# Depthwise convolution and silu moved into the input projection, and eight value-page buffers for four, in a hybrid decoder step

## The chip, the cores and the metric

The kernel runs on one core of a Trainium2 chip. The metric is the device time of one execution in microseconds, lower is better. Work is written for five engines by hand: TensorE (PE), VectorE (DVE), ScalarE (ACT), GpSimd (POOL) and SyncE (SP). Each has its own queue of instructions in program order; semaphores are the only order between queues.

## The reference

One layer of a hybrid decoder for 512 prompt tokens and 8 sample sequences of 8 tokens (576 columns, T), all in float32. The parts that the change touches:

```python
u = x @ w_in      # -> q | k | v | forget logits | z | xBC | dt | gate_att | gate_ssm
# depthwise causal convolution over 4 taps, 4096 channels; buf: the last 3 columns before
xp = concat([buf, xbc]); y = b
for j in range(4): y = y + w[j] * xp[:, j:j + l]
xbc, new_buf = silu(y), xp[:, l:]
xs, bm, cm = split(xbc)                 # 2048 | 8 groups x 128 | 8 groups x 128
y, h_new = ssd(xs, dt, a, bm, cm, h0)   # Mamba-2 state space part
m = grouped_rms_norm((y + d_skip * xs) * silu(z)) * norm_w
# sample attention reads 16 pages of 128 keys and values per sequence from a paged cache
```

Then both branches are merged through gates and an output projection, with layer norms, and PEER retrieves 128 experts per token. All states, keys, values and `new_buf` are outputs.

## The kernel before

Tensors are kept transposed: 128 channels on the partitions, 576 tokens along a row. `build` (L2397) runs four stages one after another, each in a block of its own: `project_and_prompt` (L95), `mamba_and_samples` (L653), `front` (L1356) and `peer`.

**Projection.** `u` is made in 97 tiles of 128 channels. A tile's weights (1 MB) are loaded by SP into a ring of four, ScalarE rounds them (L345), DVE takes the remainder (L470), TensorE makes 96 matmuls of 288 columns (L246), and ScalarE and DVE evict one half each (L357, L476) into a ring of four `out` buffers, which GpSimd stores to `uT` in DRAM (L620). The first 17 tiles (misc, q, k) are written out; the other 80 run in 4 rounds of 20 slots, body(r, t). In four slots of five a step of prompt attention lies between the products: scores (L277), mask and maximum on DVE (L542 to L546), exponential on ScalarE (L402), division on DVE (L554), transposes and values (L285, L295). On DVE a slot is: maximum, weight remainder, division, eviction. On ScalarE: exponential, rounding of the next weights, copy of transposes, head loads, eviction. The convolution isn't done here.

**Fused stage.** Eight groups g of the Mamba part (chunks c of 128 tokens) are interleaved by hand with the attention of sample sequence g. Per group SP loads four raw tiles (two of x, one of B, one of C, `load_raw` L791), the running sums, z and the old state, double-buffered by g % 2. DVE makes the edges of the sample sequences (`conv_edges` L909) and convolves the four tiles of group g + 1 one at a time at fixed places inside group g (`conv` L922): tile 2 ahead of `after_matrix(g, 2)`, tile 3 after `after_matrix(g, 4)`, tile 0 between the sample states 1 and 2, tile 1 ahead of `mean_square(g)`. ScalarE's `conv` (L1146) does silu of these tiles in that order, then silu of z, and only then the scaling of the attention output (L1189), for which TensorE's `turn_out` (L1322) waits. TensorE's order within a group is: scores of 16 key pages (L1281) among the chunks' products (L1222 to L1234), transposes (L1291), values 0 to 3 (L1306), chunk 4, values 4 to 7, sample states 0 and 1 (L1246), values 8 to 11, sample states 2 and 3, values 12 to 15, the square sums (L1255), `turn_out`, and the first scores of the next group (L1264).

GpSimd gathers pages of 512 KB by indirect DMA: six buffers for keys (RK), four for values (RV). Its order is

```python
for c in range(RK, PAGES): page_k(b, c)
for c in range(8): page_v(b, c)
if more:
    for c in range(RK): page_k(b + 1, c)
for c in range(8, PAGES): page_v(b, c)
```

and a gather waits until its buffer's last page is used (`k_used`, `v_used`).

## Time and profile before

| | us |
|---|---|
| median of 3 runs | 5410.88 (5408.63 to 5411.28) |
| the profiled execution | 5412.87 |
| its span, first to last instruction | 5411.1 |
| projection, from the first product to the last head's output | 13.4 to 1484.6 |
| fused stage | 1498 to 2192 |
| merge stage | 2192 to 2968 |
| PEER | 2968 to 5411 |

| engine | busy us | share of the span |
|---|---|---|
| TensorE | 4053.6 | 75% |
| VectorE | 3325.7 | 61% |
| ScalarE | 849.1 | 16% |
| GpSimd | 1463.3 | 27% |

The page cuts the span into 40 slices of 135 us. Each digit is a busy share in tenths; PEclk is the granted TensorE clock in tenths.

```profile
PE   9999999999957777899999999999999900000000
DVE  2322222222257766433452897878879789999998
PEclk9999999999967777899999999999999955555555
DMA  4332323232177876534564999999999999999998
```

The projection fills the first eleven slices, with TensorE full; the fused stage is slices 11 to 16, where no engine is full.

### The profile page before, as it was taken

What the parts mean: (1) busy time and instruction counts of PE and PEld (TensorE: products, weight loads), DVE (VectorE), ACT (ScalarE), POOL (GpSimd) and SP (SyncE); (2) the same over time, 40 slices, a digit from 0 to 9 for tenths busy, and PEclk for the clock granted to TensorE, in tenths of its full rate; (3) what the DMA queues carried; (4) which work ended last, traced back from release to release, by engine and by line L of the source; (5) the groups of instructions that cost most, each with busy time, mean ns of one, the idle gap of its engine ahead of it and who ended that gap; (6) DMA issues with size and microseconds to landing.
All of it is one profiled execution on the core that took longest, in us unless ns stands there. A gap on an engine that the chain in (4) does not pass through costs nothing. (4 is left out here: it accounts for less than half of the span.)

```text
span 5411.1 us, 60657 instructions
## 1 busy us (share of the span) xinstructions
PE 4053.6 (75%) x24165; PEld 3236.8 (60%) x24165; DVE 3325.7 (61%) x4454; ACT 849.1 (16%) x1210; POOL 1463.3 (27%) x1609
## 2 busy tenths in 40 slices
PE   9999999999957777899999999999999900000000
PEld 7999999999935545798798555555555500000000
DVE  2322222222257766433452897878879789999998
ACT  2212221212112222322352000000000000000000
POOL 0000000000043333000010122222222367777774
PEclk9999999999967777899999999999999955555555
DMA  4332323232177876534564999999999999999998
GB/s 156 117 126 100 106 100 105 100 106 100 57 254 271 289 278 241 196 110 169 173 211 161 355 419 419 398 418 421 421 420 419 421 379 410 410 410 409 410 410 331
DMA packets 336652, 1462.02 MB, mean 270 GB/s; under 512 B 84452, under 2 KB 113028, under 8 KB 196600
## 3 DMA queue, kind: packets, MB, share of 16 engines
q0 software_dynamic: 174304, 995.20, 46.1%
q1 hardware_dynamic: 131304, 430.86, 22.0%
q10 hardware_dynamic: 30768, 32.11, 1.8%
q8 instruction: 194, 3.18, 0.2%
q14 instruction: 82, 0.67, 0.0%
HBM read 1362.71 MB, written 94.75 MB: 269 GB/s over the span
## 5 line engine op out<-in xcount | busy, mean ns | idle before, releaser
L2231 DVE SCALAR_TENSOR_TENSOR i_acc<-i_row,i_cf,i_acc 128x2048 f32<-128x2048 f32 x571 | 1344.8, 2355 | 156.1 <-DMA i_row<-in_expert_v,i_ei 119.3
L2038 PE MATMUL i_p_h<-i_xT,i_ut 128*128 128x384 f32 x4096 | 1322.4, 486 | 0.0
L2038 PEld LDWEIGHTS i_p_h<-i_xT,i_ut 128*128 128x128 f32 x4096 | 779.1, 190 | 540.9 <-issue 0.6
L2347 POOL DMA_INDIRECT i_row<-in_expert_v,i_ei x576 | 544.9, 946 | 633.7 <-DVE i_acc L2231 512.2
L246 PE MATMUL a_acc<-a_xh,a_wh 128*128 128x288 f32 x3104 | 672.2, 298 | 18.1 <-DVE a_xl L466 13.4
L246 PE MATMUL a_acc<-a_xh,a_wl 128*128 128x288 f32 x3104 | 665.2, 296 | 0.0
L246 PE MATMUL a_acc<-a_xl,a_wh 128*128 128x288 f32 x3104 | 664.8, 296 | 0.0
L246 PEld LDWEIGHTS a_acc<-a_xh,a_wh 128*128 128x128 f32 x3104 | 499.2, 189 | 29.6 <-issue 26.0
L2222 DVE CUSTOM_DVE_ANT_0 i_row<-i_row,i_acc 128x2048 f32<-128x2048 f32 x192 | 433.5, 2286 | 125.1 <-DMA i_row<-in_expert_u,i_ei 123.3
L246 PEld LDWEIGHTS a_acc<-a_xl,a_wh 128*128 128x128 f32 x3104 | 500.4, 189 | 0.0
L246 PEld LDWEIGHTS a_acc<-a_xh,a_wl 128*128 128x128 f32 x3104 | 500.3, 189 | 0.0
L476 DVE COPY a_out<-a_acc 128x288 f32<-128x288 f32 x97 | 44.4, 457 | 732.8 <-PE a_acc L246 732.8
L470 DVE TENSOR_TENSOR a_wl<-a_w,a_wh 128x2048 fp32r<-128x2048 f32 x105 | 240.7, 2292 | 300.4 <-ACT a_wh L345 183.5
L2352 POOL DMA_INDIRECT i_hs<-tmp_Ha,i_hx x384 | 369.2, 961 | 117.5 <-issue 117.5
L1704 DVE TENSOR_TENSOR f_wl<-f_w,f_wh 128x1024 fp32r<-128x1024 f32 x176 | 207.7, 1221 | 221.2 <-ACT f_wh L1592 219.6
L2347 POOL DMA_INDIRECT i_row<-in_expert_u,i_ei x192 | 182.3, 949 | 560.4 <-DVE i_hs L2222 454.8
L620 POOL DMA_DIRECT2D tmp_uT<-a_out x80 | 43.7, 546 | 1040.4 <-DVE a_out L476 1026.0
L2070 ACT COPY i_ho<-i_p_h 128x384 f32<-128x384 f32 x128 | 61.2, 478 | 1248.8 <-PE i_p_h L2038 1248.8
L1592 ACT CAST f_wh<-f_w 128x1024 fp32r<-128x1024 f32 x176 | 176.1, 1049 | 379.6 <-PE f_acc L1516 210.6
L875 POOL DMA_INDIRECT e_kr<-in_cache_k,e_ik x128 | 128.1, 1001 | 201.7 <-PE e_ps L1281 173.7
L882 POOL DMA_INDIRECT e_vr<-in_cache_v,e_ik x128 | 121.2, 947 | 198.2 <-PE e_ps L1306 174.1
L357 ACT COPY a_out<-a_acc 128x288 f32<-128x288 f32 x80 | 31.9, 398 | 820.6 <-PE a_acc L246 820.6
(310 smaller groups left out, 5450.9 us busy)
## 6 DMA issues: line engine op xcount, KB each, us to landing
i_ut<-in_u_tiles SPq DMA_DIRECT2D x128, 1024.0 KB, 9.7
a_w<-in_w_in SPq DMA_DIRECT2D x97, 1024.0 KB, 4.8
f_w<-in_w_out SPq DMA_DIRECT2D x32, 1024.0 KB, 5.1
f_w<-in_w_query SPq DMA_DIRECT2D x32, 1024.0 KB, 5.2
tmp_uT<-a_out POOLq DMA_DIRECT2D x97, 288.0 KB, 2.4
tmp_Ha<-i_ho ACTq DMA_DIRECT2D x128, 192.0 KB, 9.2
f_w<-in_w_bs SPq DMA_DIRECT2D x16, 1024.0 KB, 4.9
c_csb<-tmp_cs SPq DMA_DIRECT2D x32, 288.0 KB, 5.8
```

The costliest lines, as they stand in the source:

```text
L246: last = nc.tensor.matmul(acc[:, 2 * slot + h, 0:HALF], weights[:, wslot, k * P:(k + 1) * P], x[:, k, h * HALF:(h + 1) * HALF], start=(k = ...
L470: v.tensor_tensor(wl[:, it % 2, :], w[:, it % RING, :], wh[:, it % 2, :], ALU.subtract).then_inc(w_split, 1)
L875: pool.indirect_dma_start(kr[:, n % RK, :], None, io["cache_k"], bass.IndirectOffsetOnAxis(ik[:, n:n + 1], axis=0)).then_inc(k_in[n % RK], 16)
L882: pool.indirect_dma_start(vr[:, n % RV, :], None, io["cache_v"], bass.IndirectOffsetOnAxis(ik[:, n:n + 1], axis=0)).then_inc(v_in[n % RV], 16)
L1592: nc.scalar.copy(wh[:, i % 2, h * W // 2:(h + 1) * W // 2], w[:, i % RW, h * W // 2:(h + 1) * W // 2]).then_inc(wh_out, 1)
L1704: last = v.tensor_tensor(wl[:, i % RW, part], w[:, i % RW, part], wh[:, i % 2, part], ALU.subtract)
L2038: last = nc.tensor.matmul(p_h[:, e % 2, 0:ND], ut[:, e % RU, k * P:(k + 1) * P], xT[:, k, :], start=(k == 0), stop=(k == KT - 1))
L2070: nc.scalar.copy(ho[:, m, :], p_h[:, e % 2, 0:ND]).then_inc(h_out, 1)
L2222: v.tensor_tensor_reduce(row[:, m % R, :], row[:, m % R, :], acc, 1.0, 0.0, ALU.mult, ALU.add, hs[:, j, k:k + 1]).then_inc(row_used, 1)
L2231: v.scalar_tensor_tensor(acc, row[:, m % R, :], cf[:, j, k:k + 1], acc, ALU.mult, ALU.add).then_inc(row_used, 1)
L2347: pool.indirect_dma_start(row[:, m % R, :], None, table, bass.IndirectOffsetOnAxis(index, axis=0)).then_inc(row_in[m % R], 16)
L2352: pool.indirect_dma_start(hs[:, j, k:k + 1], None, h_flat, bass.IndirectOffsetOnAxis(hx[:, j, k:k + 1], axis=0)).then_inc(pick_in[w % 2], 16)
```

## The change

The convolution, its bias and silu are taken out of the fused stage and done in the projection as soon as a tile is evicted. The tiles of `u` are put in another order for that: the 32 convolved tiles and the 48 others are dealt to the 20 slots of a round, eight convolved (t % 5 is 1 or 3) and twelve plain (`tile_of`). For a convolved tile SP also loads taps, bias and old columns of its 128 channels; DVE convolves from `out` into a new double buffer `cv`; ScalarE does silu at the end of the next slot; GpSimd stores the finished tile to `xcT` and the last columns to `convT`, and no longer stores the raw tile. The fused stage loads finished tiles straight into `xc2`, and its DVE, ScalarE and SP lose the convolution's work and waits. Apart from this, the ring of value pages there has eight buffers for four; the order of gathers is the same.

```diff
-MISC, Q0, K0, Z0, X0, B0, C0, GA0, GS0 = 0, 1, 9, 17, 33, 49, 57, 65, 81
+MISC, Q0, K0, X0, B0, C0, Z0, GA0, GS0 = 0, 1, 9, 17, 33, 41, 49, 65, 81
...
+    CONV = [t for t in range(SLOTS) if t % 5 in (1, 3)]
+    PLAIN = [t for t in range(SLOTS) if t % 5 not in (1, 3)]
+    tile_of = lambda r, t: X0 + 8 * r + CONV.index(t) if t in CONV else Z0 + 12 * r + PLAIN.index(t)
...
+        cv = sb("f_cv", [P, 2, T])
+        cp = sb("f_cp", [P, 4, 5 + 3 * NB])
+        samp = sb("f_samp", [P, NB, 3 + TB])
+        tail = sb("f_tail", [P, 2, 3 + 3 * NB])
...
-                with sp.Fori(0, ROUNDS) as r:
-                    for t in range(SLOTS):
-                        it = FIRST + V_ITEMS + t
-                        sp.wait_ge(w_split, SLOTS * r + it - RING + 1)
-                        sp.dma_start(w[:, it % RING, :], io["w_in"][ds(SLOTS * r + FIRST + t, 1)].rearrange("a p k n -> (a p) (k n)")
-                                     ).then_inc(w_in[it % RING], 16)
+
+                def body(r, t):
+                    it = FIRST + V_ITEMS + t
+                    sp.wait_ge(w_split, SLOTS * r + it - RING + 1)
+                    sp.dma_start(w[:, it % RING, :], io["w_in"][ds(tile_of(r, t), 1)].rearrange("a p k n -> (a p) (k n)")
+                                 ).then_inc(w_in[it % RING], 16)
+                    if t in CONV:
+                        c = CONV.index(t)
+                        if type(r) is not int or c >= 4:
+                            sp.wait_ge(conv_sum, 8 * r + c - 3)
+                        sp.dma_start(cp[:, c % 4, :], io["conv_par"][ds(8 * r + c, 1)].rearrange("a p n -> (a p) n")
+                                     ).then_inc(cp_in[c % 4], 16)
+                rounds(sp, body)
...
+                def silu(r, c):
+                    act.wait_ge(conv_sum, 8 * r + c + 1)
+                    nc.scalar.activation(cv[:, c % 2, :], cv[:, c % 2, :], ACT.Silu).then_inc(conv_out, 1)
...
                         load_head(4 * r + k, k, r)
+                    if t - 1 in CONV:
+                        silu(r, CONV.index(t - 1))
                     evict_late(r, t)
...
+                def conv(r, t):
+                    c = CONV.index(t)
+                    slot = (FIRST + t) % RING
+                    raw, xc, par4 = out[:, slot, :], cv[:, c % 2, :], cp[:, c % 4, :]
+                    tap = lambda j: par4[:, j:j + 1]
+                    sv = xc[:, TP:T].rearrange("p (b t) -> p b t", t=TB)
+                    rv = raw[:, TP:T].rearrange("p (b t) -> p b t", t=TB)
+                    dve.drain()
+                    dve.wait_ge(copied_a, SLOTS * r + FIRST + t + 1)
+                    dve.wait_ge(cp_in[c % 4], 32 * r + 16 * (c // 4) + 16)
+                    if type(r) is not int or c >= 2:
+                        dve.wait_ge(x_stored, 8 * r + c - 1)
+                    v.tensor_copy(samp[:, :, 0:3], par4[:, 5:5 + 3 * NB].rearrange("p (b c) -> p b c", c=3))
+                    v.tensor_copy(samp[:, :, 3:3 + TB], rv)
+                    v.tensor_copy(tail[:, c % 2, 0:3], raw[:, TP - 3:TP])
+                    v.tensor_copy(tail[:, c % 2, 3:3 + 3 * NB].rearrange("p (b c) -> p b c", c=3), rv[:, :, TB - 3:TB])
+                    v.tensor_scalar(xc[:, 0:TP], raw[:, 0:TP], tap(3), par4[:, 4:5], ALU.mult, ALU.add)
+                    dve.drain()
+                    v.tensor_scalar(sv, samp[:, :, 3:3 + TB], tap(3), par4[:, 4:5], ALU.mult, ALU.add)
+                    for j in range(3):
+                        i = 3 - j
+                        dve.drain()
+                        v.scalar_tensor_tensor(xc[:, i:TP], raw[:, 0:TP - i], tap(j), xc[:, i:TP], ALU.mult, ALU.add)
+                        last = v.scalar_tensor_tensor(sv, samp[:, :, j:j + TB], tap(j), sv, ALU.mult, ALU.add)
+                    last.then_inc(conv_sum, 1)
...
                     evict(FIRST + t, r)
+                    if t in CONV:
+                        conv(r, t)
...
+                    if late and tau - FIRST in CONV:
+                        pool.wait_ge(conv_sum, 8 * r + CONV.index(tau - FIRST) + 1)
+                        pool.sem_inc(stored[tau % RING], 16)
...
+                def store_conv(r, c):
+                    pool.wait_ge(conv_out, 8 * r + c + 1)
+                    tl.hold(pool, "a_pool")
+                    pool.dma_start(dr["xcT"][ds(8 * r + c, 1)].rearrange("a p n -> (a p) n"), cv[:, c % 2, :]).then_inc(x_flight, 16)
+                    tl.hold(pool, "a_pool")
+                    pool.dma_start(dr["convT"][ds(8 * r + c, 1)].rearrange("a p n -> (a p) n"), tail[:, c % 2, :]).then_inc(x_flight, 16)
+                    pool.wait_ge(x_flight, 32 * 8 * r + 32 * c + 32)
+                    pool.sem_inc(x_stored, 1)
+
                 def body(r, t):
+                    if t - 1 in CONV:
+                        store_conv(r, CONV.index(t - 1))
                     store(FIRST + t, r)
...
-    GC = 24
-    RK, RV = 6, 4
+    GC = 4
+    RK, RV = 6, 8
...
-                def load_raw(g):
-                    sp.dma_start(raw[:, 0:2, :], dr["uT"][X0 + 2 * g:X0 + 2 * g + 2].rearrange("a p n -> p a n")).then_inc(raw_in, 16)
-                    for j, t0 in ((2, B0), (3, C0)):
-                        sp.dma_start(raw[:, j, :], dr["uT"][t0 + g]).then_inc(raw_in, 16)
-                    sp.dma_start(old[:, :, :, :].rearrange("p a b c -> p (a b c)"), io["conv_old"][g]).then_inc(raw_in, 16)
+                def load_xc(g):
+                    k = g % 2
+                    sp.dma_start(xc2[:, k, 0:2, :], dr["xcT"][2 * g:2 * g + 2].rearrange("a p n -> p a n")).then_inc(xc_in[k], 16)
+                    for j, t0 in ((2, B0 - X0), (3, C0 - X0)):
+                        sp.dma_start(xc2[:, k, j, :], dr["xcT"][t0 + g]).then_inc(xc_in[k], 16)
...
-                sp.wait_ge(padded, 1)
-                sp.dma_start(dr["convT"][0], tail[:, :, :].rearrange("p a n -> p (a n)")).then_inc(tail_st, 16)
-                sp.wait_ge(conv_sum, 4)
-                load_raw(1)
+                load_xc(1)
                 for g in range(8):
                     k = g % 2
-                    if g < 7:
-                        sp.wait_ge(padded, g + 2)
-                        sp.dma_start(dr["convT"][g + 1], tail[:, :, :].rearrange("p a n -> p (a n)")).then_inc(tail_st, 16)
                     sp.wait_ge(u_free, 4 * g + 4)
                     sp.dma_start(dr["ssm_pT"][g], hT[:, k, :]).then_inc(h_st, 16)
                     sp.dma_start(dr["ssm_sT"][g], h0[:, k, :, :]).then_inc(s_st, 16)
                     if g < 6:
                         load_sums(g + 2)
                     if g < 6:
-                        sp.wait_ge(conv_sum, 4 * g + 8)
-                        load_raw(g + 2)
+                        load_xc(g + 2)
...
-                conv_edges(0)
-                dve.wait_ge(gc_in, 16)
-                for a in range(4):
-                    conv(0, a)
                 query(0)
                 forget_sums()
                 dve.wait_ge(const_in, 128)
...
                     segments(g, 1)
-                    if g < 7:
-                        conv_edges(g + 1)
                     after_matrix(g, 0)
...
                     segments(g, 3)
-                    if g < 7:
-                        conv(g + 1, 2)
                     after_matrix(g, 2)
...
                     after_matrix(g, 4)
-                    if g < 7:
-                        conv(g + 1, 3)
                     for u in range(2):
                         sample_states(g, u)
-                    if g < 7:
-                        conv(g + 1, 0)
                     for u in range(2, 4):
                         sample_states(g, u)
                     gated(g)
-                    if g < 7:
-                        conv(g + 1, 1)
                     mean_square(g)
...
-                def conv(g):
+                def gate(g):
                     k = g % 2
-                    xc = xc2[:, k, :, :]
-                    for i, a in enumerate((2, 3, 0, 1) if g else range(4)):
-                        act.wait_ge(conv_sum, 4 * g + i + 1)
-                        nc.scalar.activation(xc[:, a, :], xc[:, a, :], ACT.Silu).then_inc(conv_out, 1)
                     act.wait_ge(loaded[k], NLOAD * (g // 2) + NLOAD)
                     nc.scalar.activation(z[:, k, :, :], z[:, k, :, :], ACT.Silu).then_inc(z_out, 1)
...
-                        conv(g + 1)
+                        gate(g + 1)
...
-                        pe.wait_ge(conv_out, 4 * g + 4)
+                        pe.wait_ge(xc_in[g % 2], 48 * (g // 2) + 48)
...
-    w_all = np.concatenate([misc, q, k, z, xbc, ga, gs], axis=1)
-
-
-    def group4(w):
-
-        t = w.reshape((32, P) + w.shape[1:])
-        pick = np.array([[2 * g, 2 * g + 1, 16 + g, 24 + g] for g in range(SG)])
-        return np.moveaxis(t[pick], 2, 1)
+    w_all = np.concatenate([misc, q, k, xbc, z, ga, gs], axis=1)
```

The functions `conv_edges` and `conv` of the fused stage's DVE are removed; names of parameters and outputs follow.

## Rows read from the trace of the kernel before

**Rows 1.** Waits of TensorE, fused stage, then group 4: engine line <- releaser: total us, times, longest.

```profile
PE e_ps L1306 <- DMA e_vr<-in_cache_v,e_ik: 49.8, 41, 5.3
PE e_ps L1322 <- ACT e_ov L1189: 25.7, 7, 3.7
...
PE e_ps L1306 <- DMA e_vr<-in_cache_v,e_ik: 5.9, 5, 4.2
```

**Rows 2.** Timeline of DVE (start us, us, work, [idle before <-releaser]), first work of groups.

```profile
1532.28 0.16 DVE L1044 TENSOR_TENSOR e_sn<-e_ps,e_maskn 128x8 f32<-128x8 f32 x1
...
1623.63 0.17 DVE L1044 TENSOR_TENSOR e_sn<-e_ps,e_maskn 128x8 f32<-128x8 f32 x1 [2.94 <-PE e_ps L1265]
...
2114.42 0.17 DVE L1044 TENSOR_TENSOR e_sn<-e_ps,e_maskn 128x8 f32<-128x8 f32 x1 [1.72 <-PE e_ps L1265]
```

**Rows 3.** Timeline of TensorE in group 4.

```profile
1810.45 1.06 PE L1234 MATMUL c_p_s<-c_xst,c_btok 128*128 128x256 f32 x2
...
1832.57 0.64 PE L1306 MATMUL e_ps<-e_vr,e_pT 128*32 128x256 f32 x8
...
1845.89 2.27 PE L1306 MATMUL e_ps<-e_vr,e_pT 128*32 128x256 f32 x16 [4.25 <-DMA e_vr<-in_cache_v,e_ik]
...
1859.04 1.24 PE L1255 MATMUL c_p_cb<-c_mo,c_ones 128*128 128x288 f32 x4 [0.66 <-DVE c_mo L1012]
...
1864.93 0.69 PE L1322 MATMUL e_ps<-c_ident,e_ov 128*128 128x128 f32 x2 [3.67 <-ACT e_ov L1189]
```

**Rows 4.** Windows: us, busy PE, PEld, DVE, ACT, POOL; granted clock, DMA share, GB/s.

```profile
1787.83:1869.39 81.56, 62.61 (x579) 42.03 (x580) 58.34 (x181) 20.70 (x36) 30.13 (x32) 0.75 0.80 280
...
1837.80:1847.80 10.00, 5.64 (x28) 2.93 (x24) 7.07 (x24) 0.88 (x2) 5.22 (x6) 0.50 1.02 411
```

**Rows 5.** Timeline of DVE in one slot of the projection.

```profile
863.55 0.46 DVE L476 COPY a_out<-a_acc 128x288 f32<-128x288 f32 x1 [8.03 <-PE a_acc L246]
...
869.89 0.35 DVE L554 TENSOR_SCALAR d_pr<-d_pr,d_sm 128x256 f32<-128x256 f32 x1
...
878.09 0.46 DVE L476 COPY a_out<-a_acc 128x288 f32<-128x288 f32 x1 [7.25 <-PE a_acc L246]
```

**Rows 6.** Timeline of DVE in group 4: one convolution, what follows it, the squares.

```profile
1809.61 0.54 DVE L926 TENSOR_SCALAR c_xc<-c_raw,c_gc 128x512 f32<-128x512 f32 x1
...
1813.36 0.42 DVE L977 TENSOR_TENSOR c_t<-c_p_yo,c_csj 128x256 f32<-128x256 f32 x1
...
1857.63 1.36 DVE L1012 TENSOR_TENSOR c_mo<-c_z 128x1152 f32<-128x1152 f32 x1
```

**Rows 7.** Timeline of ScalarE in group 4.

```profile
1862.78 0.68 ACT L1151 ACTIVATE c_xc<-c_xc 128x576 f32<-128x576 f32 x1 [14.54 <-DVE c_xc L932]
```

**Rows 8.** Timeline of GpSimd in group 4: the gathers of values 4 and 8.

```profile
1826.83 0.93 POOL L882 DMA_INDIRECT e_vr<-in_cache_v,e_ik  x1 [17.58 <-PE e_ps L1306]
...
1839.29 0.94 POOL L882 DMA_INDIRECT e_vr<-in_cache_v,e_ik  x1 [0.30 <-issue]
```

**Rows 9.** Timeline of TensorE in group 7, which has no convolution.

```profile
2157.47 1.94 PE L1306 MATMUL e_ps<-e_vr,e_pT 128*32 128x256 f32 x16
2160.46 1.08 PE L1306 MATMUL e_ps<-e_vr,e_pT 128*32 128x256 f32 x8 [1.05 <-DMA e_vr<-in_cache_v,e_ik]
...
2180.86 2.29 PE L1255 MATMUL c_p_cb<-c_mo,c_ones 128*128 128x288 f32 x4
```

**Rows 10.** Timeline of DVE in group 7: the squares.

```profile
2176.62 1.36 DVE L1012 TENSOR_TENSOR c_mo<-c_z 128x1152 f32<-128x1152 f32 x1
```

**Rows 11.** Timeline of DVE at the start of the fused stage: the forget sums.

```profile
1525.57 4.43 DVE L1038 TENSOR_TENSOR_SCAN e_rev<-e_one,e_lf 128x2048 f32<-128x2048 f32 x1 [3.32 <-DMA e_lf<-in_cache_f,e_il]
```

**Rows 12.** Timeline of TensorE in group 0.

```profile
1554.72 2.08 PE L1222 MATMUL c_p_yo<-c_mm,c_xpad 128*128 128x128 f32 x8 [3.77 <-DVE c_mm L968]
```

**Rows 13.** Groups by line, fused stage: name, count, busy us, mean ns, idle before.

```profile
L1151 ACT ACT_TABLE_LOAD x8 | 10.3, 1283 | 17.0 <-PEq L194 16.8
...
L915 DVE COPY c_samp<-c_raw 128x64 f32<-128x64 f32 x32 | 6.5, 220 | 0.0
```

70 lines of the change are left out of this document (23 added, 47 removed).

## The prediction

> **What bounds the kernel now.** I read the forty slices first. The program has four stages one after another: input projection with prompt attention, the fused stage of Mamba and sample attention, the merge stage, and PEER, which ends the run (their limits stand in the table above). The diff touches the first two; what they lose or gain passes unshortened to the end, as every stage starts when the one before has finished.
>
> In the fused stage I took the waits of TensorE [rows 1], then the periods of the eight groups: the first DVE instruction of a group starts at 1532.28, 1623.63 (group 1) and 2114.42 (group 7) [rows 2], so groups 1 to 6 take (2114.42 - 1623.63)/6 = 81.8 us each and group 0 takes 91.3. Then I read one period, group 4, engine by engine. The reader is to see that no engine bounds it all; it is a chain that changes hands. In its first half DVE is the late one (scores, masks, convolution, norm of the group before), in its second half TensorE is, and it idles three times: for value pages, for DVE's squares, and 3.67 us for ScalarE's scaled output [rows 3]. DMA is busy 0.80 of the period, and in a full stretch of 10 us it moves 411 GB/s [rows 4].
>
> In the projection a slot (one 128-column tile) runs from one eviction to the next, 863.55 to 878.09, 14.54 us, and DVE is through with all that the next slots need 6.69 us after the start (869.89 + 0.35 - 863.55); then it idles 7.25 us for TensorE [rows 5]. TensorE bounds this stage.
>
> **The change, part by part.**
>
> *Convolution out of the fused stage.* Per group DVE loses four convolutions and the edge copies. One convolution runs from 1809.61 until the next work at 1813.36, 3.75 us [rows 6]. What that is worth depends on its place:
> - Channel tile 2 stands ahead of the work that waits for TensorE's state product, which is over at 1810.45 + 1.06 = 1811.51 [rows 3]; DVE comes to it at 1813.36 [rows 6]. So 1.85 us of the 3.75 is on the path; the rest becomes a wait. Bounds 0 and 1.85; I take 1.85, since TensorE's next product waits for DVE's matrix.
> - Tiles 3 and 0 and the edge copies stand ahead of waits for TensorE that exist already: worth 0, and their cover is TensorE's second half.
> - Tile 1 stands ahead of the mean square. ScalarE's silu of that tile starts at 1862.78 after a 14.54 us wait [rows 7], and the silu of z and the scaling of the output are queued behind it. TensorE waits 3.67 us for that scaling [rows 3], 25.7 us in 7 groups [rows 1]. Afterwards ScalarE does z early and scales as soon as the values are summed: 3.67 us per group go. Next late is TensorE's own square sum, which already ends there; so the whole 3.67 counts.
>
> *Eight value buffers for four.* GpSimd gathers in the order: values 0 to 7, six key pages of the next group, values 8 to 15. With four buffers values 4 to 7 are issued only from 1826.83, after 17.58 us without a free buffer, the six key pages follow, and value 8 goes out at 1839.29 [rows 8]. TensorE wants it at 1841.6 and gets it at 1845.89, a 4.25 us wait [rows 3]. With eight buffers values 4 to 7 and the key pages go out in those 17.58 idle us, and value 8 needs only value 0 to be used, which is what releases the gather of 1826.83 now; so it leaves some 12 us earlier than at 1839.29, where 4.25 are missing. All waits for value pages are 49.8 us in 41 places [rows 1], 6.2 us per group. I count all of them, bounds 0 and 6.2.
>
> *Matmuls after the waits.* The stretch 1837.8 to 1847.8 has a granted clock of 0.50, the lower level of 1.2 GHz, with that wait in it [rows 4]. Group 7 has no 4.25 us wait. From the second batch of its value matmuls to the end of DVE's squares: 2176.62 + 1.36 - 2157.47 = 20.51 us, of which 1.05 was waiting for a page [rows 9, 10], so 19.5. In group 4: 1857.63 + 1.36 - 1832.57 = 26.42 [rows 3, 6], of which 5.9 was waiting for pages [rows 1], so 20.5. I add 1.0 per group; bounds 0 and the rival below.
>
> *Sum per period:* 1.85 + 3.67 + 6.2 + 1.0 = 12.7 us, so 81.8 becomes 69.1; six periods give 76.3.
>
> *Group 0.* At the start four convolutions stand before the forget sums, but these wait another 3.32 us for the last forget page at 1525.57 [rows 11]: worth 0, hidden by sixteen gathers. Then TensorE waits 3.77 us at 1554.72 for DVE [rows 12], which is held by the second group's edge copies and their late load. That wait is gone: 12.7 + 3.8 = 16.5.
>
> *Group 7.* No convolution in it. The square sum starts at 2180.86 after late value pages, while DVE's squares end at 2177.98 and would end 1.05 earlier [rows 9, 10]: 3.9 us.
>
> *SP's queue in the fused stage.* Each group loses the store of tails, the old rows and two waits for DVE; the loads of four tiles stay, finished ones now, and leave some 3 us earlier behind the free state buffer. They fill the other half of a double buffer, needed a period later: 0.
>
> *Convolution into the projection.* Eight of twenty slots per round, 32 in all. DVE gets 3.75 us plus four small copies (mean 0.22 in the trace, overlapping) [rows 13], about 4.6 us with the added drain. Its wait for ScalarE's half of the eviction is nothing, both evict at once. Behind it on DVE are the mask and maximum of the next attention step, behind these ScalarE's exponential and weight rounding, then DVE's weight remainder and the probabilities. So the 6.69 us become 11.3, against a slot of 14.54 [rows 5]: 3.2 us of cover left, cost 0. At the other place (slot 3 of 5) the next slot has no attention step, so less is behind it. ScalarE gets a silu and two table loads of 1.28 us per tile [rows 13], after its rounding and before an eviction it waits for anyway: 0. On SP each 14.5 KB parameter load follows a weight load and waits for a convolution four tiles back, long done. On GpSimd two stores and one landing per convolution tile come before the next tile's store; four output buffers cover them. GpSimd then stores 12 raw tiles per round for 20. Cost of the whole: 0 to 5 us over the stage (its first round and its end), I take 1.
>
> *Total:* 76.3 + 16.5 + 3.9 - 1 = 96 us. The profiled execution took 5412.87 (span 5411.1) and the median is 5410.88; 96 off gives 5317 for a profile and 5315 for the median.
>
> **The rivals.**
>
> *DMA becomes the bound of the group.* 0.80 of 81.56 us is 65.2 us of DMA work per group [rows 4]; in 69.1 it is a share of 0.94. For: the loads of SP and the gathers come closer together, and there is hardly room for gaps. Against: by bytes it is only 280 x 81.56 / 411 = 56 us. It decides if the work can't be packed above 0.90: then the period is 72.5, and six periods give 56 for 76.3, groups 0 and 7 some 3 less: 5338.
>
> *The clock comes back wholly.* Without waits the second half could run at 2.4 GHz. The mean granted clock of group 4 is 0.75 over 62.61 busy us of TensorE [rows 4]; at the upper level throughout a quarter of that, 15.7 us, is the far bound. Most of it lies where DVE is the late one, so I estimate a quarter of it as gain, 4 us per period: 30 us more off, 5285. Against: in group 7, without the long wait, the stretch gained 1.0 only.
> The Trainium skill, page "TensorE: Matmul & The Clock Gate", section "HAM oscillation — how this bites in real kernels", lays repeated low clock in a loop to DMA waits between batches of matmuls. By that the removal of the waits would bring this rival's time; the trace agrees in part, since 0.50 is granted in the stretch with the wait, but the clock was low there before the wait, too.
>
> *The buffers don't help.* If a value page is late because of DMA and not of its issue, the 6.2 us per group and the 1.0 stay: 7 x 7.2 + 3.9 = 54 us less gain, 5369. Against: GpSimd's idle 17.58 us.
>
> *Slower: the DVE queue in the projection holds up TensorE.* If a convolution takes C us there, TensorE stalls C - 7.85 (14.54 - 6.69) in each of 16 slots. It costs nothing up to 7.85 and eats the whole gain of 97 from C = 14 (7.85 + 97/16). A wait at its head could do it: for its parameters, or for GpSimd's store two tiles back, with everything named above queued behind. With C = 15 the time is 5411 + 16 x 7.15 - 97 = 5428. Against: both are due several slots earlier.
> On this the Trainium skill, page "SBUF — State Buffer", section "Who interferes with whom", says that a DVE tensor_scalar in its two-port mode and a GpSimd instruction block each other fully. By that a convolution could grow by GpSimd's issue of 0.5 to 1 us for each of its two such instructions, still under 7.85, so it only makes this rival a little less unlikely.
>
> **How the numbers follow.** Forecast as summed (5301 to 5329) 0.67; DMA bound 0.15; clock 0.10; buffers don't help 0.05; slower 0.03. The likeliest gives 5315. The range leaves out the last two and the tails: 5280 to 5348. About 0.2% is what a measurement of this kernel can tell from no change. All cases but the last are faster by far more: faster 0.96, same 0.01, slower 0.03.
>
> **What would show it.** The projection still ends near 1485, slots of 14.5 us, no TensorE wait for DVE. Starts of groups 69 us apart. GpSimd without the 17.6 us gap before value 4, no TensorE wait over 1 us for value pages, none for the scaled output. Wrong would be: a period over 73 with DMA share over 0.9 (first rival), a granted clock near 1.00 throughout and a period under 66 (second), value waits as before (third), waits of TensorE on DVE in the projection (fourth).

## The result and the profile after

The changed kernel takes 5271.01 us (median of 4 runs, 5260.49 to 5280.38) against 5410.79: ratio 0.9742, 95% interval 0.972 to 0.9764. The forecast was 5315 with 5280 to 5348. The sign was right, but 140 us came off in place of 96, outside the range. The profiled execution took 5260.49 us (span 5258.6), 152.5 less than that of before.

The groups are marked by the first work of each on VectorE, as in [rows 2]; here those of groups 0, 1 and 7 (start us, us, work, [idle before <-releaser]):

```profile
1524.39 0.16 DVE L1072 TENSOR_TENSOR e_sn<-e_ps,e_maskn 128x8 f32<-128x8 f32 x1
...
1591.20 0.17 DVE L1072 TENSOR_TENSOR e_sn<-e_ps,e_maskn 128x8 f32<-128x8 f32 x1 [0.70 <-PE e_ps L1276]
...
1973.22 0.17 DVE L1072 TENSOR_TENSOR e_sn<-e_ps,e_maskn 128x8 f32<-128x8 f32 x1 [0.70 <-PE e_ps L1276]
```

| part of the span | before | after | gain | forecast |
|---|---|---|---|---|
| until group 0 starts | 1532.3 | 1524.4 | 7.9 | -1 |
| group 0 | 91.3 | 66.8 | 24.5 | 16.5 |
| groups 1 to 6, each | 81.8 | 63.7 | 18.1 | 12.7 |
| group 7, to its transposed output | 70.4 | 60.5 | 9.9 | 3.9 |

The six periods give 108.8 us together, and all rows 151 of the 152.5. Waits of TensorE in the whole fused stage, as in [rows 1]:

```profile
PE e_ps L1292 <- DMA e_kr<-in_cache_k,e_ik: 28.9, 25, 4.4
...
PE c_p_yo L1233 <- DVE c_mm L996: 16.0, 10, 3.2
...
PE c_p_cb L1266 <- DVE c_mo L1040: 13.0, 7, 2.9
PE e_ps L1317 <- DMA e_vr<-in_cache_v,e_ik: 9.2, 17, 1.3
```

Waiting for value pages took 49.8 us before and takes 9.2 now. The scaled output cost 25.7 before and has no row now. The masked matrix of VectorE (`c_mm`) cost 41.0 before, in 15 waits. Seven of these were of 1.83 to 1.93 us, one in a group, such as this one ahead of the third chunk's products of group 4 before:

```profile
1817.52 1.16 PE L1222 MATMUL c_p_yo<-c_mm,c_xpad 128*128 128x128 f32 x8 [1.92 <-DVE c_mm L968]
```

Now 16.0 us are left in 10 waits. In group 4 GpSimd issues value 8 at 1821.55 with a gap of 1.42 us, the transposed output comes without a wait, and the next scores of new tokens take 1.85 us, 3.42 before (as [rows 3, 8]):

```profile
1821.55 0.98 POOL L936 DMA_INDIRECT e_vr<-in_cache_v,e_ik  x1 [1.42 <-PE e_ps L1317]
```

```profile
1834.48 0.64 PE L1317 MATMUL e_ps<-e_vr,e_pT 128*32 128x256 f32 x8 [0.57 <-DMA e_vr<-in_cache_v,e_ik]
...
1843.79 1.87 PE L1266 MATMUL c_p_cb<-c_mo,c_ones 128*128 128x288 f32 x4 [1.89 <-DVE c_mo L1040]
1845.46 2.12 PE L1266 MATMUL c_p_s<-c_mo,c_ones 128*128 128x288 f32 x4
1847.38 0.53 PE L1333 MATMUL e_ps<-c_ident,e_ov 128*128 128x128 f32 x2
1847.74 1.85 PE L1275 MATMUL e_ps<-e_kn,e_qp 128*128 128x8 f32 x16
```

Next comes one window over six periods, now marked by TensorE's transposed output, from that of group 0 to that of group 6. By this mark the six take 110.2 us less. Columns as in [rows 4]. Before:

```profile
1619.17:2111.43 492.26, 374.89 (x3468) 252.56 (x3469) 349.26 (x1080) 124.21 (x211) 182.93 (x192) 0.75 0.78 276
```

After:

```profile
1588.78:1970.80 382.02, 324.14 (x3469) 228.12 (x3468) 255.20 (x792) 107.23 (x183) 182.43 (x192) 0.87 0.95 356
```

The same matmuls (3468 and 3469 records) keep TensorE busy 50.8 us less (374.9 to 324.1), and its idle time falls by 59.5 (117.4 to 57.9). So nearly half of the gain stands in TensorE's busy time and not in its waits. The granted clock rose from 0.75 to 0.87, and clock times busy time is the same before and after: 0.75 x 374.9 = 281 and 0.87 x 324.1 = 282. It is the same work at a higher clock. This is a split of TensorE's time; what each part of the change brings is read from the experiments. The groups by line of that window say which matmuls became faster (count, busy us, mean ns, idle before). Before:

```profile
L1306 PE MATMUL e_ps<-e_vr,e_pT 128*32 128x256 f32 x768 | 82.5, 553 | 39.6 <-DMA e_vr<-in_cache_v,e_ik 38.6
...
L1246 PE MATMUL c_p_s<-c_xst,c_bmask 64*128 64x256 f32 x48 | 24.9, 672 | 0.0
...
L1264 PE MATMUL e_ps<-e_kn,e_qp 128*128 128x8 f32 x96 | 20.5, 352 | 0.0
```

After:

```profile
L1317 PE MATMUL e_ps<-e_vr,e_pT 128*32 128x256 f32 x768 | 64.2, 472 | 10.6 <-DMA e_vr<-in_cache_v,e_ik 7.9 <-ACT e_pT L1191 2.6
...
L1257 PE MATMUL c_p_s<-c_xst,c_bmask 64*128 64x256 f32 x48 | 17.0, 483 | 0.0
...
L1275 PE MATMUL e_ps<-e_kn,e_qp 128*128 128x8 f32 x96 | 11.5, 256 | 0.0
```

### The profile page after: what moved, and what is told of

Its sections match the earlier page's. It is cut to its first block and busy times, and to the rows that moved or that the text cites. A ratio compares the mean times of both kernels' runs of the same rounds, so it can differ in the third digit from the quotient of the medians.

```text
span 5258.6 us, 61057 instructions
## 1 busy us (share of the span) xinstructions
PE 3984.0 (76%) x24165; PEld 3204.5 (61%) x24165; DVE 3327.4 (63%) x4454; ACT 933.3 (18%) x1274; POOL 1476.5 (28%) x1641
## 3 DMA queue, kind: packets, MB, share of 16 engines
q0 software_dynamic: 175328, 995.65, 46.9%
q1 hardware_dynamic: 133608, 430.42, 22.9%
## 5 line engine op out<-in xcount | busy, mean ns | idle before, releaser
L1512 PE MATMUL f_acc<-f_x1l,f_wh 128*128 128x256 f32 (+1 forms) x512 | 151.6, 296 | 0.0
L364 ACT CAST a_wh<-a_w 128x2048 fp32r<-128x2048 f32 x79 | 149.9, 1898 | 4.0 <-POOLq L684 4.0
```

What stands on the lines that cost most here:

```text
L364: nc.scalar.copy(wh[:, it % 2, :], w[:, it % RING, :]).then_inc(wh_out, 1)
L1512: last = nc.tensor.matmul(acc_of, stationary, moving, start=(k == first_k and t == 0), stop=(k == last_k and t == 2))
```

## The experiments

They ran on several chips, and by the time of the kernel before these are of two kinds: on one the kernel before takes 5410 to 5413 us, on the other 5464 to 5466. I call them chips A and B. Each kernel is held against the kernel before on its own chip.

| kernel | chip | us | ratio to before, interval |
|---|---|---|---|
| changed, again | A | 5268.4 | 0.9738 (0.9722 to 0.9754) |
| changed, again | B | 5382.0 | 0.9833 (0.9807 to 0.9858) |
| convolution moved alone | A | 5335.3 | 0.9867 (0.985 to 0.9883) |
| the same | B | 5395.0 | 0.9872 (0.9855 to 0.9888) |
| buffers, VectorE's convolution put back | A | 5313.3 | 0.9826 (0.9809 to 0.9842) |
| the same | B | 5395.8 | 0.9872 (0.9855 to 0.9888) |

**Each part alone.** The changed kernel with four value buffers:

```diff
-    RK, RV = 6, 8
+    RK, RV = 6, 4
```

> The changed kernel with four value buffers again: the convolution moved, alone. Theory C (the convolution is worth its path and the scaling, the clock comes back only when the value waits go): per period 1.85 + 3.67 less, the 4.25 us wait ahead of value 8 still there, granted clock of a group about 0.75, periods near 76 us, total 5355 to 5370. Theory S (the two parts are independent and it was the convolution that held the clock down): periods near 70, clock over 0.85, total near 5320.

> The changed kernel with four value buffers: the convolution moved alone, again, in case this chip is the one on which the kernel before takes 5411 us (the first run of it was where that takes 5465). There the whole change takes 64.1 us a period against 83.2. Theory S (the two parts need each other: the matmuls of the second half stay at the slow level as long as either wait is there): 74 to 78 us a period, 50 to 75 us under the kernel before, so that the parts' gains sum to less than the whole's 140. Theory A (each part gives its own): the sum of the two is 140 within 15. On the other chip: 69 us again.

The changed kernel with VectorE's convolution work put back, into a row that nobody reads, at the old places and also four times at the start. Called "buffers alone" below, it isn't quite that: the silus on ScalarE and the copies of the edges stay out, so it lacks the wait for the scaled output too.

```diff
                     after_matrix(g, 4)
+                    if g < 7:
+                        conv(g + 1, 3)
...
                         sample_states(g, u)
+                    if g < 7:
+                        conv(g + 1, 0)
```

> Buffers alone, as far as the VectorE's time goes: the changed kernel, in which VectorE also makes the old convolution's instructions (two tensor_scalar and six scalar_tensor_tensor of each value tile) at the old places in its queue, four tiles ahead of the first query and four in each group, into a row that nobody reads; the silu on ScalarE and the copies of the edges stay out. So it adds work and leaves none out. Theory 1 (VectorE's queue cost little of the gain: one tile on its chain of 1.85 us in six periods, the start, group 0): 11 us for the six periods, 13 for the start where the wait for the log decays covers it in part, so 10 to 30 us slower than the changed kernel. Theory 2 (the two halves need each other: every wait in the middle of a group lets the clock fall and costs double): 40 to 70 us slower than the changed kernel, about the sum that the convolution moved alone gave (69 us). The granted clock of the fused stage tells them apart: above 0.85 by theory 1, 0.80 or less by theory 2.

> Buffers alone as far as VectorE's time goes, again on this chip: eight value buffers, and VectorE also makes the old convolution's instructions at the old places, into a row that nobody reads. Theory S: 73 to 77 us a period, 50 to 75 us under the kernel before. Theory A: what the kernel with four value buffers leaves of 140 us. Forecast's own terms: 6.2 us of page waits and 3.67 of the scaled output in six periods, so 75 to 80 us under the kernel before. On the other chip: 70 us again.

Measured on chip A, the two kernels are 74 us and 96 us faster than before, in sum 171, and both parts together give 140 to 143. The 74 lie in theory S's range, with a period a little under its 74 to 78 (72.8, table below); the 96 lie above every range named. The sum is 31 us more than the whole, but two gains are in both kernels and so counted twice. One is the wait for the scaled output, 25.7 us before and without a row in either. The other is an earlier start of the fused stage: VectorE's first work there is at 1492.6 and 1492.3, against 1498.4 before. Together they are about the excess, so these runs don't show that the parts take anything from each other on chip A.

On chip B it is 69, 70 and 84, an excess of 55, more than these two explain. The first run with the move alone fell between its theories C and S there, with C's period (75.8). The one with the convolution put back is 14 us slower than the changed kernel, in the range of its theory 1, while the granted clock of 0.82 in its fused stage (1590 to 2010 us) is between what the two theories asked for.

The parts of the period on chip A follow, as means of six periods in us. They are cut at the first rows of four lines in TensorE's timeline: transposed output, first turn (the transposes of the probabilities), first value matmul, square sums.

| kernel | output to turn | to values | to square sums | to output | period |
|---|---|---|---|---|---|
| before | 39.0 | 3.3 | 33.9 | 5.9 | 82.0 |
| convolution moved alone | 33.8 | 3.2 | 33.4 | 2.4 | 72.8 |
| buffers alone | 36.4 | 3.4 | 26.0 | 4.0 | 69.8 |
| changed | 33.2 | 3.1 | 24.5 | 2.9 | 63.7 |

The convolution's move shortens the first part and the wait for the output; the buffers shorten the value part by 7.9. TensorE's busy time in the same periods, in us per period, shows where each part brings the clock back (windows over all six):

| kernel | output to turn | turn to square sums |
|---|---|---|
| before | 30.6 | 29.7 |
| convolution moved alone | 26.6 | 29.2 |
| buffers alone | 28.4 | 22.9 |
| changed | 26.8 | 24.4 |

In the second part, where the value pages are waited for, the faster matmuls come with the buffers alone. In the first part most of it comes with the move. Theory S had the second half slow as long as either wait is there; that isn't so. For group 4, turn to square sums, in the order of the table (columns as in [rows 4], the clock is the third number from the end):

```profile
1822.13:1859.04 36.91, 29.97 (x209) 16.13 (x209) 22.67 (x77) 8.02 (x18) 16.90 (x18) 0.63 0.77 278
...
1854.23:1890.84 36.61, 32.36 (x209) 18.92 (x210) 15.24 (x60) 7.51 (x17) 16.87 (x18) 0.58 0.76 280
...
1849.41:1878.59 29.18, 22.57 (x209) 14.84 (x209) 22.39 (x76) 12.63 (x23) 8.96 (x9) 0.85 0.78 312
...
1817.36:1843.79 26.43, 21.96 (x209) 12.96 (x210) 15.18 (x60) 8.88 (x18) 9.71 (x11) 0.94 0.91 371
```

The window of six periods and the waits of the stage, convolution moved alone:

```profile
1600.69:2037.54 436.85, 349.15 (x3470) 234.07 (x3468) 255.13 (x792) 110.12 (x187) 181.67 (x192) 0.80 0.87 313
```

```profile
PE e_ps L1317 <- DMA e_vr<-in_cache_v,e_ik: 49.7, 30, 6.6
```

Buffers alone:

```profile
1599.99:2019.01 419.02, 331.73 (x3470) 240.76 (x3468) 340.43 (x984) 109.26 (x186) 187.39 (x192) 0.84 0.89 324
```

```profile
PE c_p_cb L1291 <- DVE c_mo L1055: 44.7, 8, 6.6
PE c_p_yo L1258 <- DVE c_mm L1011: 36.7, 15, 3.7
```

TensorE is busy 374.9 us before, 349.2 with the move, 331.7 with the buffers, 324.1 with both. So the buffers carry the larger share of the clock. And once pages are on time, VectorE's squares, with the convolutions of tiles 3 and 0 in the queue ahead of them, are late: TensorE waits 44.7 us for them, 6.0 us in the kernel before. So the cover that the forecast gave these two tiles, TensorE's second half, is gone once that half is faster, and their move is worth something beside the buffers.

**Only the clock.** The kernel before, with 13 matmuls that nobody reads ahead of value page 8, where TensorE waits:

```diff
                     sample_states(g, 1)
+                    filler(13)
                     values(g, 2)
```

> The kernel before with 13 extra matmuls (128 x 96, to 96 PSUM columns that nobody reads) ahead of value 8, where TensorE waits 4.25 us: TensorE works in the wait, everything else as it was. Theory C: the granted clock rises in the stretch after the wait, the values, sample states and first scores of the next group run in half their time, periods fall by 2 to 5 us, total 5370 to 5395. Theory D (those matmuls are slow because of late pages or DVE, the clock follows and doesn't lead): periods the same or 0 to 1 us longer, total 5408 to 5420.

It takes 5463.35 against 5464.27 on chip B, ratio 0.9998 (0.9989 to 1.0008): by time, theory D. TensorE in one group (the trace has two records for each filler matmul):

```profile
1854.75 4.91 PE L1239 MATMUL c_p_cb<-c_ident 128*128 128x96 f32 x26
1859.59 1.93 PE L1310 MATMUL e_ps<-e_vr,e_pT 128*32 128x256 f32 x32
1861.45 1.13 PE L1250 MATMUL c_p_s<-c_xst,c_bmask 64*128 64x256 f32 x4
...
1864.81 0.64 PE L1310 MATMUL e_ps<-e_vr,e_pT 128*32 128x256 f32 x8 [1.36 <-DMA e_vr<-in_cache_v,e_ik]
1867.63 1.08 PE L1310 MATMUL e_ps<-e_vr,e_pT 128*32 128x256 f32 x8 [2.19 <-DMA e_vr<-in_cache_v,e_ik]
```

With its idle time filled, TensorE does the next 32 value matmuls in 1.93 us, the upper level, where [rows 3] show 2.27 for 16. So theory C has its first step right. But TensorE then waits for the next pages and gains nothing. Over six periods it is busy 398.0 us, of which 26.1 are filler; that leaves 371.9, against 390.3 in the kernel of the next experiment on the same chip, and the six periods take 500.4 and 502.7 us. With four buffers faster matmuls only meet later pages.

**Only the scaled output.** The kernel before, with the scaling put ahead of the silus of tile 1 and z on ScalarE:

```diff
                     for i, a in enumerate((2, 3, 0, 1) if g else range(4)):
+                        if g and i == 3:
+                            scale_out(g - 1)
```

> The kernel before with one order changed on ScalarE: the scaling of the attention output stands ahead of the silu of the last convolved tile and of z, not behind them. The 3.67 us term alone. My sum: TensorE's wait for the scaled output goes, but the mean square and the silu of tile 1 behind the convolution still hold the next group's first transposes back, so 2 to 3.67 us per period, total 5385 to 5397. Rival: the wait only moves to the next group's first transposes, which need silu of tile 1: 0 to 1 us per period, total 5403 to 5411.

It takes 5458.95 us, ratio 0.9988 (0.9979 to 0.9998): 5 us, in the rival's range. The 3.67 us wait is gone, but VectorE's segment sums now idle 27 us, 0.9 before. The profile puts 12.4 of them down to ScalarE's queue and the rest to nothing that it shows. That they wait for exponentials which stand behind the silus fits the order of the queue and isn't shown further. Waits of VectorE there:

```profile
DVE c_seg L940 <- issue: 14.6, 4, 4.1
DVE c_seg L940 <- ACTq L1169: 12.4, 3, 4.1
```

**The point from which the projection stalls.** The changed kernel with each convolution made two or three times:

```diff
-                    v.tensor_scalar(xc[:, 0:TP], raw[:, 0:TP], tap(3), par4[:, 4:5], ALU.mult, ALU.add)
...
+                    for _ in range(3):
+                        dve.drain()
+                        v.tensor_scalar(xc[:, 0:TP], raw[:, 0:TP], tap(3), par4[:, 4:5], ALU.mult, ALU.add)
```

> The changed kernel in which VectorE makes the convolution of each tile of the projection three times over (same result, two thirds of it work added): about 12 us in place of 4 beside each of the 32 value tiles and key tiles' slots. The forecast put the point from which the projection stalls at 7.85 us of convolution per slot. If it holds: TensorE waits for VectorE's copy some 4 us in each of 24 to 32 slots, 100 to 130 us slower than the changed kernel, projection's end at 1580 to 1610 us in place of 1483. Rival (the copy's queue position or a second accumulator hides more): within 20 us of the changed kernel.

> The changed kernel in which VectorE makes the convolution of each tile of the projection twice over (same result, one half of it work added). Three times over cost 118 us of time and 126 us at the projection's end, where the forecast's threshold of 7.85 us of convolution per slot gave 133 for 32 slots. Twice over is 8.2 us, 0.3 to 0.4 over it: 10 to 15 us slower than the changed kernel by the threshold. Rival (the threshold is met only where a slot's copy comes late, and other waits take the rest): under 5 us. Rival (the cost runs in proportion from the first convolution, 59 us for each): 50 to 60 us slower.

Three times takes 5389.6 us, 119 to 121 over the changed kernel on chips A. Twice takes 5290.3, 22 over it on the same chip. VectorE's last copy of the projection starts at 1483.0, 1509.9 and 1609.1 us for one, two and three convolutions. TensorE's waits in the projection, three times over:

```profile
PE a_acc L304 <- DVE d_pr L579: 73.8, 16, 5.6
PE a_acc L265 <- DVE a_wl L495: 13.5, 13, 1.3
```

At the projection's end a third convolution costs 99 us, a second 27, the first nothing. So the stall begins where the forecast put it, at some 8 us, and in 16 slots. My expectation with 24 to 32 slots had its total right by luck: 16 waits give 74 us, the 13 for the weights' remainder (`a_wl`) 13.5, and slower matmuls (busy 1499.8 us to 1610, against 1461.2 to 1483 in the changed kernel) 39 more. A second convolution costs more than the 10 to 15 us expected: of its 27 us 8.0 are these 16 waits and 9.5 slower matmuls (busy 1470.7 to 1510).

**Is the DMA the bound now?** The changed kernel with 1.8 MB less in a period: it loads and stores one sample state in eight, and leaves the others out of its output:

```diff
-                    sp.dma_start(h0[:, k, :, :], io["ssm_old"][g]).then_inc(loaded[k], 16)
+                    sp.dma_start(h0[:, k, 0:(8 if g < 2 else 1), :], io["ssm_old"][g][:, 0:(8 if g < 2 else 1), :]).then_inc(loaded[k], 16)
...
-                    sp.dma_start(dr["ssm_sT"][g], h0[:, k, :, :]).then_inc(s_st, 16)
+                    sp.dma_start(dr["ssm_sT"][g][:, 0:1, :], h0[:, k, 0:1, :]).then_inc(s_st, 16)
```

> The changed kernel with less traffic: of the sampled states only one of the eight samples of a group is stored, and from group 2 on only one is loaded (128 KB each way in place of 1024 KB); the rest of that output is left out and those products work on old data, all instructions of the engines stay. That is 1.8 MB of about 22.5 MB in a period. Theory D (in the changed kernel the DMA engines bound the period): at the 320 to 360 GB/s of its busy stretches 5 to 5.6 us a period, 30 to 40 us in all. Theory E (chain of waits and clock bound it, the DMA share follows from that): under 2 us a period, within 12 us in all.

It takes 5278.22 us, ratio 0.9755 (0.9738 to 0.9771) on chip A, where the changed kernel has 0.9738 and 0.9742: no gain, theory E. The DMA share falls to 0.90 and the periods are 64.3 us:

```profile
1587.39:1972.97 385.58, 326.61 (x3470) 237.34 (x3469) 254.43 (x792) 109.22 (x187) 182.94 (x192) 0.86 0.90 325
```

**Chip B.** 

> The changed kernel itself, nothing edited, as the reference for the kernels beside it. The single move of the convolution with four value buffers gave 69 us on a chip where the kernel before takes 5464 us (shares of the DMA engines 0.85 in its fused stage). Theory 'pages and clock together': the eight buffers add the other half, so the sum is 130 to 150 us under the kernel before of the same chip, granted clock of the fused stage 0.85 to 0.92. Rival 'the DMA engines are what is left': on a chip with slower transfers the gain is cut, to 80 to 110 us, with their share at 0.90 or more and waits for keys in every group.

> The kernel before, nothing edited, for its trace on the chip of these runs: where that chip spends the 54 us that it took longer (5465 against 5411 us), and what a group of the fused stage takes there. With the filler added, a kernel of the same time had a mean period of 83.7 us on it, against 83.2 on the first chip. Theory: the fused periods are as long as on the first chip (83 to 84 us; page waits and slow clock set them), and the 54 us are in other stages; then the changed kernel's gain on this chip (84 us) is smaller because its own periods are longer there (75.1 against 64.1 us), since only the changed kernel asks the DMA engines for all they have. Rival: the fused stage of the kernel before is longer as well, by 5 us a period or more.

The second of these ran once, on a chip A (5411.18 us, periods 81.7), so it says nothing of chip B. How long the periods of the kernel before are on B rests on two kernels made from it, that with filler (83.4) and that with the scaling first (83.8), against 82.0 on A. The changed kernel takes 5382.0 on B. The gain of 84 us is in the rival's range of 80 to 110, but its DMA share of 0.86 is under the 0.90 that the rival named, so the rival isn't shown. The same window there:

```profile
1602.68:2047.96 445.28, 361.43 (x3469) 257.86 (x3468) 254.64 (x792) 110.46 (x188) 182.12 (x192) 0.81 0.86 307
```

Its periods are 74.2 us, the time from output to turn is 44.6 in place of 33.2, and inside the fourth batch of scores TensorE has gaps of 0.3 to 1.1 us between matmuls, for which the profile shows no releaser. In the last stage VectorE idles 191 us ahead of its accumulation there and 158 in the repeat on A. What the profile puts down to late rows is about the same (120 and 122 us); 40 more on B have no releaser shown. The packets of the software queue, which carries the gathers, take 46.7% of 5380 us there and 46.9% of 5265 on A for the same 996 MB, nearly 2% more time. So slower transfers are likely on B, and not shown to be the cause. Whether late key pages or the clock (0.81) come first in the fused stage is not settled; the run with less traffic fell on a chip A.

**Other depths, other places.** Seven key and seven value buffers (RK, RV = 7, 7), and the reciprocal of the norm moved behind the next group's second segment:

> The changed kernel with seven key buffers and seven value buffers in place of six and eight, the same bytes in all. The changed kernel's TensorE waits 28.9 us in 25 waits for pages of keys, and 9.2 us in 17 for pages of values. Theory 1 (the pages' depth is spent: with DMA shares of 0.91 to 0.98 a buffer only moves a wait from one kind of page to the other): within 8 us of the changed kernel. Theory 2 (values are served late because their pages come free late, as with four buffers): keys' waits fall by 5 to 15 us, and those for values rise by less; 5 to 15 us faster. Theory 3 (eight value buffers are needed for the run of eight issues back to back): 10 to 25 us slower, with the value waits back in the second half of the group.

> The changed kernel with one instruction moved: the reciprocal of the norm (3.75 us on VectorE by the changed kernel's profile, about ahead of which TensorE waits 3.2 us for the products and 1.9 us for the output matrix) leaves the path between the norm and the first output and goes behind the second segment of the next group. Theory 1 (VectorE's chain ends last at these places): 2 to 4 us a period less, 12 to 25 us in all. Theory 2 (the DMA engines' pages set the period, share 0.91 to 0.98): within 5 us of the changed kernel, the waits for keys grow by what the waits for VectorE lose.

On chip B, beside 5382.0 for the changed kernel: 5406.6 with seven and seven, 25 slower, theory 3; GpSimd waits 101.1 us for value buffers in place of 55.7 (1600 to 2050 us). The moved reciprocal gives 5375.0, 7 less with overlapping intervals: between its theories.

**Filler on top of the change.**

```diff
+                    if c == 2:
+                        filler(8, e_ps[:, 3, 0:96])
                     pe.wait_ge(m_out, ck + 1)
...
+                    if u == 0:
+                        filler(6)
                     pe.wait_ge(e_out, 5 * b + u + 1)
...
                 def square_sums(g):
+                    filler(8)
                     pe.wait_ge(sq_out, g + 1)
```

> The changed kernel with matmuls whose result nobody reads, put on TensorE into its three waits of a group: eight ahead of the third segment's products (wait for the masked matrix of 2.6 to 3.3 us), six ahead of the first turn (1.4 to 2.0 us for the exponentials), eight ahead of the square sums (1.9 to 2.6 us for the output). They add work and leave none out. Ahead of four buffers the filler gained nothing, since pages were late by as much. Theory 1 (with eight value buffers the clock's gain is kept): scores of the new tokens 1.9 instead of 3.4 us, turns 2.7 instead of 3.5, square sums 3.5 instead of 4.4, less 0 to 1 us for filler that outlasts its wait: 1.5 to 3.5 us a period, 10 to 25 us in all. Theory 2 (pages bound the period): no change within 5 us, waits for keys grow by what the matmuls lose. Theory 3 (filler outlasts the waits): 5 to 15 us slower.

> The changed kernel with the filler matmuls in TensorE's three waits of a group, again, now beside the changed kernel on the same chip. It took 5256.7 us where the changed kernel had taken 5271 us on a like chip, with intervals that overlap. Theory 1 (the clock's gain is kept in part): 5 to 20 us under the changed kernel. Theory 2 (no more than noise, since the period fell only from 63.7 to 63.0 us): within 5 us of it.

> The changed kernel with both: the reciprocal of the norm moved behind the next group's second segment, and the filler matmuls in the three waits. The reciprocal alone gave 7 us (5375 against 5382 us, intervals overlapping), and takes most of the wait ahead of the third products away, so the eight fillers there are in the path. If the two gains are of different places: 15 to 30 us under the changed kernel. If the DMA engines bound the period: 5 to 10 us under it. If the filler outlasts the shortened wait: 5 us over it to 5 us under.

It takes 5256.7 us, and beside the changed kernel on one chip 5249.2 (0.9697, 0.9681 to 0.9713) against 5268.4 (0.9738, 0.9722 to 0.9754): 19 us, with intervals apart, theory 1. With the moved reciprocal it takes 5261.4: nothing added. The filler kernel is the fastest that ran. The profile of the second run is of an execution of 5262.35 us, the slowest of its four and only 4 us under the changed kernel's profiled one (5266.51):

```profile
1589.40:1975.20 385.80, 347.81 (x3733) 259.05 (x3732) 254.97 (x792) 109.21 (x187) 181.75 (x192) 0.88 0.95 354
...
L1299 PE MATMUL e_ps<-e_kr,e_qp 128*32 128x128 f32 x1536 | 57.2, 297 | 24.1 <-DMA e_kr<-in_cache_k,e_ik 24.1
...
L1265 PE MATMUL c_p_cb<-c_ident 128*128 128x96 f32 x168 | 23.3, 295 | 0.0
...
L1265 PE MATMUL e_ps<-c_ident 128*128 128x96 f32 x96 | 11.5, 274 | 0.0
```

Without the 23.3 + 11.5 = 34.8 us of filler TensorE is busy 313.0 us, 12.2 less than in the changed kernel's run beside it (325.2 in its six periods). Its idle time and the filler make 72.8 us, against 62.4 idle there, and its wait for keys is 24.1 against 10.3. So the clock's gain is there, and most of it is given back in this execution, in which the six periods are 2 us shorter. The profile of the first run (5251.62 us) has six periods of 377.7 us and 311.4 of busy time without filler. How the 19 us of the medians divide is not shown.

**The start.** VectorE's first work of the fused stage, before and after; its last copy of the projection starts at 1483.93 and 1483.03:

```profile
1498.35 0.48 DVE L1075 MEMSET c_xpad<- 128x512 f32 x1 [13.74 <-PEq L194]
```

```profile
1490.36 0.48 DVE L1103 MEMSET c_xpad<- 128x512 f32 x1 [6.64 <-PEq L206]
```

> The kernel before, with the transfers of its projection issued by SyncE in the form of the changed kernel (first round written out, then a loop over the other rounds), nothing else edited. The changed kernel's fused stage begins 7.1 us earlier than the kernel before's, measured at VectorE's first memset (1490.4 against 1498.4 us), while the projection ends only 0.9 us earlier. Theory L (SyncE's loop form is the cause): the memset at 1490 to 1492 us. Theory N (another cause, such as what the engines have to load at the end of the projection): it stays at 1497 to 1499 us. The total moves by no more than 8 us in either case.

It takes 5410.26 us, with the memset at 1498.79: theory N. SyncE's loop form isn't it. In that gap nothing runs in either kernel but the issue and transfer of the last head's output, and its cause stays open. With VectorE's convolutions back, the four at the start too, group 0 begins at 1526.6, as it does with them moved and four buffers (1526.6): they are worth nothing there, as forecast.

## Why the prediction was wrong in size

- **Matmuls after the waits, 1.0 us per period: the step that failed.** The six periods show 50.8/6 = 8.5 us less busy time. I had taken the 1.0 from group 7 against group 4, since group 7 has no 4.25 us wait. But group 7 runs mostly at the lower level itself: the granted clock is 0.58 in its stretch (2157.47 to 2177.98 us) and 0.55 in that of group 4 (1832.57 to 1858.99). Its 8 value matmuls take 1.08 us [rows 9], and the same 8 take 0.64 in the changed kernel. I compared slow with slow. The work in the two stretches wasn't equal either: 105 matmul records in group 7's and 121 in group 4's, since the last 8 value matmuls of group 7 and the 8 for the new tokens start behind its squares. So the 1.0 says nothing of the clock.
- **The clock's rival** had the right mechanism, and its 5285 us is the nearest of the forecast's times. The period under 66 us came as it said; the clock near 1.00 didn't (0.87), so its far bound of 15.7 us wasn't reached. Its estimate of a quarter was too small; more than half came. It named the stage where VectorE is late as the place where the clock wouldn't come back; yet 3.8 us of the 8.5 came there, with the move, and 5.4 behind the turn, with the buffers, less 0.7 in the square sums. The Trainium skill, page "TensorE: Matmul & The Clock Gate", section "HAM oscillation — how this bites in real kernels", was the rule that spoke for this rival. The traces agree for the second half: with the buffers alone the value pages' waits go from 49.8 to 1.7 us, and the clock of the stretch behind the turn in group 4 from 0.63 to 0.85.
- **The waits, 1.85 + 3.67 + 6.2 = 11.7 us per period.** The idle time of TensorE fell by 59.5/6 = 9.9. The page waits went nearly as summed (value pages 38.6 to 7.9 us in the six periods, 5.1 each). The scaled output went whole, in 7 groups. The 1.85 us are there too: the wait of 1.92 us for VectorE's matrix in each group is gone or under 1 us, and all waits for that matrix fell from 31.9 to 12.0 us in the six periods (18.3 in the repeat on chip A). What I named next late, TensorE's own square sums, was not it: they now wait 1.89 us for VectorE's squares. Keys cost 22.1 us in place of 6.1, and 10.3 in the repeat.
- **The 3.67 us as a term of its own** is worth 0.8 us per group by the reordering, in which the silus stay on ScalarE. What it is worth with the silus gone no run shows alone.
- **Groups 0 and 7.** Group 0 was built from the same terms, so it missed in the same way, 24.5 for 16.5. Group 7 was built from its late squares and pages alone, with nothing for the clock, and gave 9.9 for 3.9: TensorE is busy 57.9 us in it before and 50.7 after.
- **Projection, cost 1 us:** right. TensorE has no new wait for VectorE there, the last copy comes 0.9 us earlier, a convolution takes 4.0 us there (865.18 to 869.18) where it took 3.75, and the threshold of 7.85 us is borne out by the runs with more convolutions. So the fourth rival (slower) didn't come.
- **The buffers don't help:** wrong by the value waits, 49.8 us before and 9.2 now.
- **DMA rival:** its premise, no packing above a share of 0.90, is wrong on chip A: 0.95 over six periods. Share times period was not a fixed work either: 0.78 x 82.0 = 64.0 us before, 0.95 x 63.7 = 60.5 after. On chip B the gain, 84 us, is near this rival's (73) and the period over 73, but the share is 0.86, so its other sign is missing.
- **Start, 0:** 7 us came that no step had, from the gap between the stages.

## What to carry over

A wait in a chain of matmuls can cost more than its own length, since what follows may run at the lower clock. To size that, compare the mean time of one matmul, line by line, with a stretch whose granted clock is at the upper level, and not with another group of the same kernel; count the matmuls in both stretches first. When a part is tried alone, list what else its kernel lacks before its gain is added to another's: here two kernels shared two gains, and their sum was 31 us too high. A threshold worked out from one slot's slack can be trusted where the doubled and tripled cost bears it out.

## What the hardware showed unexpectedly

The DMA engines were busy 0.95 of 382 us at 356 GB/s with gathers and plain transfers mixed. Filler in a wait raised the clock (32 value matmuls in 1.93 us) without any gain in time while pages were late; with eight buffers it gave 19 us. Chips differ: 5411 and 5465 us for the same kernel, and the same change gives 140 us on one and 84 on the other.
